# Modulation chunks 4, 5 and 6 issued at the seam between input projection and attention, in a two-layer diffusion trunk step

## The reference, cut to what matters

```python
mod = (silu(cond) @ w_mod[i] + b_mod[i])          # w_mod[i] is (1024, 6 * 1024); two rows of cond: context, latent
shift1, scale1, gate1, shift2, scale2, gate2 = mod
h = rms_norm(x, norm1_g[i]) * (1 + scale1) + shift1
qs, kvs = token_tensors(h, w_in[i], ...)          # h @ w_in[i], 1952 columns, norms and rotary
x = x + gate1 * mix(qs, kvs, ...)                 # attention: 6 latent-compressed, 6 grouped, 4 differential heads, then w_out
h = rms_norm(x, norm2_g[i]) * (1 + scale2) + shift2
x = x + gate2 * hier_moe(h, ...)                  # 16 experts, two of a group per token
```

## Time and profile before

| what | value |
|---|---|
| median of 3 runs | 1440.59 us (1439.44 to 1442.46) |
| profiled execution, span | 1439.5 us (the page gives the span alone, no time of its own beside it) |
| PE busy | 1272.5 us, 88% |
| PE weight load busy | 758.1 us, 53% |
| DVE busy | 717.1 us, 50% |
| ACT busy | 411.0 us, 29% |
| POOL busy | 212.9 us, 15% |
| all chunks of modulation (line 1763) | 1536 records in 24 chunks, 53.3 us of PE |

### The profile page before, as it was taken

How to read it: one execution, slowest core, us unless ns; L and a number is a source line. 1 busy time by engine, 2 the same in 40 slices (tenths; PEclk the granted TensorE clock), 3 DMA queues, 4 the chain that set the end, 5 groups by cost and what they waited for, 6 DMA issues and landing times. The chain is left out here.

```text
span 1439.5 us, 22597 instructions
## 1 busy us (share of the span) xinstructions
PE 1272.5 (88%) x8192; PEld 758.1 (53%) x8192; DVE 717.1 (50%) x1727; ACT 411.0 (29%) x923; POOL 212.9 (15%) x305
## 2 busy tenths in 40 slices
PE   4999989999999959998959999899999994999981
PEld 3455556777767734433435554577776673444330
DVE  0344525776744535543514554367786346355442
ACT  2111135666620111111111111556665010111111
POOL 1210013010021111221111010210101111122212
PEclk9899989999999969999969999999999997999995
DMA  9700239110041797999960004580101324899955
GB/s 348 284 14 1 97 122 334 37 31 16 2 147 59 264 382 235 355 372 351 313 184 14 0 1 175 211 202 1 31 16 64 134 80 164 310 375 376 338 197 177
DMA packets 73708, 245.19 MB, mean 170 GB/s; under 512 B 6072, under 2 KB 14753, under 8 KB 60977
## 3 DMA queue, kind: packets, MB, share of 16 engines
q1 hardware_dynamic: 56080, 183.26, 34.3%
q0 software_dynamic: 17056, 58.61, 13.9%
q10 hardware_dynamic: 432, 1.36, 0.2%
HBM read 213.87 MB, written 31.00 MB: 170 GB/s over the span
## 5 line engine op out<-in xcount | busy, mean ns | idle before, releaser
L1846 PE MATMUL ps<-ring,hT_region 128*128 128x512 f32 (+1 forms) x640 | 271.7, 581 | 3.4 <-ACT hT_region L954 3.4
L1846 PEld LDWEIGHTS ps<-ring,hT_region 128*128 128x128 f32 x640 | 121.3, 193 | 135.4 <-issue 134.8
L1316 DVE TENSOR_SCALAR_CACHE_REDUCE ring<-ps 128x768 f32<-128x768 f32 (+1 forms) x168 | 132.7, 820 | 119.9 <-PE ps L1918 92.8
L1007 ACT ACTIVATE ring<-ring,negm 128x768 f32<-128x768 f32 (+1 forms) x168 | 137.7, 820 | 31.2 <-DVE ring L1316 31.2
L2042 PE MATMUL ps<-ring,hT_region 128*128 128x384 f32 (+1 forms) x480 | 141.9, 452 | 0.0
L2184 PE MATMUL ps<-ring,hT_region 128*128 x272 | 127.4, 623 | 10.3 <-SPq L587 4.4
L1918 PE MATMUL ps<-arena,qT 64*128 64x384 f32 (+1 forms) x640 | 125.7, 507 | 8.5 <-DVE ring L1316 2.9
L2042 PEld LDWEIGHTS ps<-ring,hT_region 128*128 128x128 f32 x480 | 89.6, 190 | 42.0 <-issue 0.3
L1971 PE MATMUL ps<-work,arena 128*64 128x128 f32 x1600 | 105.5, 278 | 5.9 <-ACT work L1023 4.3
L1023 ACT ACTIVATE work<-ps 128x512 f32<-128x512 f32 x128 | 75.8, 592 | 99.2 <-PE ps L1743 99.2
L1971 PEld LDWEIGHTS ps<-work,arena 128*64 128x64 f32 x1600 | 86.1, 137 | 25.2 <-issue 15.1
(11 more groups left out here) (297 smaller groups left out, 1759.6 us busy)
## 6 DMA issues: line engine op xcount, KB each, us to landing
ring<-in_w_mod SPq DMA_DIRECT2D x24, 2048.0 KB, 11.4
ring<-in_moe_w_gate SPq DMA_DIRECT2D x32, 1024.0 KB, 11.7
ring<-in_moe_w_up SPq DMA_DIRECT2D x32, 1024.0 KB, 15.3
arena<-in_moe_w_down SPq DMA_DIRECT2D x32, 1024.0 KB, 14.4
ring<-in_w_in SPq DMA_DIRECT2D x6, 2048.0 KB, 20.6
arena<-mod_rows POOLq DMA_DIRECT2D x12, 512.0 KB, 5.8
x_rows<-x POOLq DMA_DIRECT2D x10, 512.0 KB, 3.0
h_rows<-work POOLq DMA_DIRECT2D x10, 512.0 KB, 2.9
```

The costliest lines, as they stand in the source:

```text
L1007: act.activation(v, v, ACT.Exp, bias=negm[:, 2 * (k % 3) + m:2 * (k % 3) + m + 1], scale=-1.0, accum_out=sums[:, c:c + 1]).then_inc(exp_do ...
L1316: ts(o_, i_, -pair_of(p)[4], None, ALU.mult, ALU.min, accum_out=col).then_inc(m_ready, 1)
L1846: last = mm(ps[:, b, 0:n], hT[:, c, t * P:(t + 1) * P], w[:, c, :], start=(c == 0), stop=(c == KC - 1))
```

## The change

Chunks 4, 5 and 6 leave the steps of the context tile. PE issues chunk 4 right behind the last tile's block 3, chunk 5 right behind the last `keys2`, and chunk 6 behind `queries_T(0)`. Chunk 7 moves from step 9 to step 3. ACT copies chunks 4, 5 and 6 one after the other behind `query_copy(0)`, ahead of its step 0. Two waits are added: chunk 4 (bank 1) waits until block 1 of the last tile has been read, and chunk 5 (bank 3) until all blocks have been read. The order of chunks, their banks, slots, copies and stores stay as they are.

```diff
+MOD_EARLY = 3
+
+
 def mod_of_step(k):
 
-    if k in range(3, 3 + 2 * MOD_CTX, 2):
-        return MOD_FIRST + (k - 3) // 2
+    if k == 3:
+        return MOD_FIRST + MOD_EARLY
     return MOD_LAT + MOD_STEPS.index(k) if k in MOD_STEPS else None
...
                 query_copy(0)
+                for j in range(MOD_FIRST, MOD_FIRST + MOD_EARLY):
+                    mod_copy(l, j)
                 for k in range(NP + 4):
...
                     pe.wait_ge(mod_evac, l * N_MOD + j - 1)
+                if j == MOD_FIRST:
+                    pe.wait_ge(z_used_d, l * 4 * NT + 4 * (NT - 1) + 2)
+                if j == MOD_FIRST + 1:
+                    pe.wait_ge(z_used_d, (l + 1) * 4 * NT)
+                    pe.wait_ge(z_used_a, (l + 1) * 3 * NT)
...
                     z_block(t, 3)
+                mod_chunk(l, MOD_FIRST)
                 keys1(l, NU - 1)
                 keys2(l, NU - 1)
+                mod_chunk(l, MOD_FIRST + 1)
...
                 queries_T(0)
+                mod_chunk(l, MOD_FIRST + 2)
                 for k in range(NP + 3):
```

## The result

The changed kernel takes 1423.45 us, median of 4 runs (1421.5 to 1424.13), against 1440.01 us of the kernel before (1437.63 to 1442.46, 4 runs). The ratio is 0.9872, 95% interval 0.9847 to 0.9896: 16.6 us less. I had forecast 1430.7 with a range from 1426.5 to 1437.0.

What follows compares the result with a forecast made beforehand. Seam bound by hand-overs, context tile nearly and latent tiles wholly by PE. 12.58 + 7.68 + 8.91 = 29.17 us per layer saves 3.3 and 6.6, together 9.9: span 1429.6, forecast 1430.7, range 1426.5 to 1437.0.

Steps and rivals of the forecast that it cites:

- Chunk 4 costs nothing: Seam, behind block 3: chunk 4's 1.86 us goes into PE's 2.49 us wait for the keys, cost 0.
- Chunk 6 waits: Seam, ahead of step 0: PE waits 1.8 us for ACT's copy of chunk 4, where the gap was 0.78.
- steps 4 to 9: Context tile up to `scores(10)`: three chunks (5.58 us) and a 1.32 us wait go, 15.81 becomes 8.91 us.
- The third rival: Later stages: the saving is not passed on, or one layer loses its clock and eats it; 1440.6 us, chance 0.07.
- the term for steps 0 to 3: Start of the context tile: a chunk stays at the end of step 3, so 7.68 us as before.
- 35.78 and 32.49: Old times in us from block 3's end to `scores(10)`, layers 0 and 1, from which 29.17 per layer was subtracted.
- `scores(10)`'s gain: Behind step 10 PE hardly idles, so time gained at `scores(10)` should go through to the layer's end.
- The range's low end: 1426.5 us: full clock in steps 0 to 3 (2.8) and no output-copy wait (up to 1.7).
- The gaps come back: Rival, tile: waits like the 0.84 us show where three chunks stood, 2.5 us per layer; 1435.7 us, chance 0.14.
- The clock falls and stays low: Rival, gap ahead of chunk 6 to step 10: low clock costs 6.5 us per layer; 1443.7 us, slower, chance 0.07.
- The rule of the Trainium skill: Steps 4 to 9: if it governed, removing chunks would remove what holds the clock, giving the slower rival's time.
- median 1.1 above the span: Whole kernel: the runs' median lies 1.1 us above the profiled span, so span 1429.6 gives forecast 1430.7.

Runs made afterwards that it cites:

- the opened gap: Changed kernel with chunk 4 issued behind the last `keys2`, next to chunk 5, so PE idles ahead of the keys again: 1432.87 us, ratio 0.9933 to the kernel before.
- the held-back load: Changed kernel with SP holding the load of chunk 8, and those behind it, until `scores(3)` is done: 1424.33 us, ratio 0.9875 to the kernel before.

## Why the forecast missed

**What held.** Chunk 4 costs nothing: `keys1` is where it was, in every kernel that has the chunk there, and layer 0's seam kept the full clock, as forecast. Chunk 5 delays `queries_T(0)` to +7.95 (893.53 - 885.58) against +7.87 forecast. Chunk 6 waits 1.91 us for ACT (1.8 forecast), `scores(0)` stands at +12.80 (12.58). The wait ahead of `scores(10)` is gone; steps 4 to 9 take 8.65 (8.91). In neither profile of the changed kernel did a chunk of the attention wait for its weights. The third rival fell: the gain passed through whole. From `scores(16)` to `scores(49)`, the last of the attention, it is 141.4 us in layer 0 and 141.6 in layer 1 in every profile.

**What failed, first: the term for steps 0 to 3, "7.68 us [...]. I take the same."** They took 6.29 (898.39 to 904.68). I had treated the fall of the clock in the thin steps as a property of those steps. The runs show that it depends on what stands ahead of them: with chunk 6 right before step 0, some group of steps 0 to 3 ran at the low clock in 3 of 18 stretches, counting every variant and the opened gap; without chunk 6 there, in all ten. The cleanest pair is the changed kernel, 0 of 4, against chunk 6 at step 3, 2 of 2. In the sum: 1.4 per layer, 2.8.

**Second: the durations of before, taken from one execution.** I took 35.78 and 32.49 for the layers and explained their difference by the clock, but as if each layer had its own. Over three profiles the stretch averages 35.12. No stretch of the old schedule ran at full clock throughout; my estimate for one is 32.49 less the 1.43 that steps 0 to 3 lost there, 31.06. By this estimate the clock cost the kernel before 4.06 us per layer on average, and in its two profiles the changed kernel loses none of it, beside 31.06 - 27.74 = 3.3 of schedule. My sum had the schedule's 3.3 in both layers and the clock's part in one only. This adds 1.0 per layer, 2.0.

**Third: that `scores(10)`'s gain "should go through to the end of the layer", with nothing added behind it.** Steps 10 to 15 gained 29.18 - 28.49 = 0.7 per layer on average, 1.4 in all: weights that came too late for chunks 9 and 10 by up to 0.74 us, and issue gaps and one slow group whose cause is open.

The seam came out 0.2 longer per layer and steps 4 to 9 0.3 shorter, which cancel. That leaves 9.9 + 2.8 + 2.0 + 1.4 = 16.1, beside a measured 16.6; the second measurement of the changed kernel, ratio 0.9902, comes to 14.1. The range's low end had the first of these but neither of the others.

Two smaller readings were off without changing the result. I took a chunk at the low clock as about 2.5 us; that one had run partly at full clock, and a chunk wholly at the low clock took 3.60. And the "median 1.1 above the span" compared two different executions: a run's time lies 2.2 above its own span (1422.78 and 1420.6), so the execution that I read had been about 1.1 us slower than the median.

**On the rivals.** "The gaps come back" did not come: the only wait of the kind stayed 0.65. "The clock falls and stays low" named the right mechanism with the wrong sign. The rule of the Trainium skill, "TensorE: Matmul & The Clock Gate", Part 4, that the full clock doesn't engage for transposes, would, if it governed here, have made steps 4 to 9 slow; in both profiles of the changed kernel they ran at 1.00 granted, eight query transposes among them (1.09 us). In four stretches of three variants the clock did fall in step 8, within 1 us of the end of ACT's 0.65 us wait. The transposes didn't bring it about: in each of the four, the values product just ahead of them already took 0.59 to 0.70 us instead of 0.44, as in the rows of the held-back load above. The third profile of the kernel before shows a fall at the same wait, over 4 us ahead of the transposes, which then ran at full clock. PE's timeline, layer 0:

```profile
215.04 0.54 PE L1971 MATMUL ps<-work,arena 128*64 128x128 f32 x4 [0.84 <-ACT hT_region L1028]
215.51 3.44 PE L1763 MATMUL ps<-ring,silu_c 128*2 128x128 f32 x64
...
219.67 1.09 PE L1743 MATMUL ps<-ident,arena 128*128 128x128 f32 x8
```

Why the clock falls there in some executions stays open, since the changed kernel has the same wait and kept the clock.

## What to carry to other kernels

Work that can go anywhere is worth most in the hand-over gap where TensorE would idle, and ahead of a stretch where it can only work in snatches: taking a 1.86 us chunk out of a 2.5 us gap cost some 4 us per layer by the medians, and 6.5 in the slowest run, because the clock fell as well. Price a moved piece twice, by the wait that it fills and by what the granted clock reads behind the place that it leaves and the place that it takes. Where the clock falls in the old kernel, take its durations from several executions before summing; one profile may hold its luckiest stretch. The same holds for a variant: before reading a cost from its profile, see where that execution stands among its runs.

## What was not expected of the hardware

The clock's fall has no fixed place. In the kernel before it came at the key transposes, in `keys2`, at step 1 or at step 3, with the same instructions and waits ahead of it, and single executions of one kernel spread over 10 us (1434.14 to 1444.5 in 17 runs). Chunks are slowed most: the same 64 records took 1.93, 2.54, 3.23 or 3.60 us, depending on how much of them fell into the low clock. Not every slow group is the clock, though: `scores(12)` at 2.43 instead of 1.56 us and chunks at 2.33 and 2.35 ran while it read 1.00, in windows with a DMA share over 1.
